# The dense products of a two-layer encoder: 576 tokens in parts of 304 and 272 columns in place of 288 and 288

## The reference

```python
def token_mix(xn, past, w_in, b_f, w_branch, w_gate, w_out):
    (a_q, a_k, a_v, i_q, i_k, i_w, b_q, b_k, b_v, c_q, c_k, c_v, c_f) = split(xn @ w_in)   # 1024 -> 3k columns
    ...                                                                                   # three mixers: o_a, o_b, o_c
    branch = einsum('btnw,nwd->btnd', o, w_branch)                                         # 3 x (512 -> 1024)
    gate = sigmoid((xn @ w_gate).reshape(B, T, 3, 1024))                                   # 1024 -> 3072
    return einsum('btnd,btnd->btd', gate, branch) @ w_out, new_rows                        # 1024 -> 1024

def conv_ffn(xn, conv_past, w_up, conv_w, conv_b, w_down):
    h = xn @ w_up                                                                          # 1024 -> 5632
    hc = conv_b + sum(conv_w[i] * shifted(h, i) for i in range(3))
    g, u = split(hc, 2)
    return (silu(g) * u) @ w_down, last_rows                                               # 2816 -> 1024

def trunk(x, ...):
    for l in range(2):
        x = x + token_mix(rmsnorm(x, norm_mix[l]), ...)
        x = x + conv_ffn(rmsnorm(x, norm_ffn[l]), ...)
    return rmsnorm(x, norm_final), new_state
```

## Time and profile before

| what | value |
|---|---|
| median of three timed runs | 2106.25 us |
| the profiled execution: span from first to last instruction | 2104.0 us |
| mean granted TensorE clock | 0.999 of 2.4 GHz |
| PE busy | 2086.9 us, 99% of the span, 15926 matmuls |
| PE weight loads | 1983.6 us, 94% |
| DVE, ACT, POOL busy | 66%, 48%, 11% |
| DMA | 175.05 MB, 83 GB/s on average |

### The profile page before, as it was taken

How to read it: one execution, slowest core, us unless ns; L and a number is a source line. 1 busy time by engine, 2 the same in 40 slices (tenths; PEclk the granted TensorE clock), 3 DMA queues, 4 the chain that set the end, 5 groups by cost and what they waited for, 6 DMA issues and landing times.

```text
span 2104.0 us, 39764 instructions
## 1 busy us (share of the span) xinstructions
PE 2086.9 (99%) x15926; PEld 1983.6 (94%) x15934; DVE 1395.2 (66%) x2612; ACT 1006.0 (48%) x1635; POOL 228.9 (11%) x162
## 2 busy tenths in 40 slices
PE   8999999999999999999999999999999999999998
PEld 8898988898999999999998989889989999999998
DVE  7669637878747763676465895488787377637753
ACT  6267325647626652444352672255475266424432
POOL 0022000000041110011310220000001301001112
PEclk9999999999999999999999999999999999999999
DMA  6231222121122222222232212221211222222222
GB/s 203 77 106 41 91 81 96 51 81 51 61 81 81 80 90 91 90 80 90 91 108 81 93 44 93 78 96 51 81 51 61 81 89 81 90 91 80 90 85 93
DMA packets 53764, 175.05 MB, mean 83 GB/s; under 512 B 6720, under 2 KB 11408, under 8 KB 53632
## 3 DMA queue, kind: packets, MB, share of 16 engines
q1 hardware_dynamic: 47168, 158.88, 24.0%
q0 software_dynamic: 2688, 9.95, 1.2%
q10 hardware_dynamic: 3776, 4.34, 0.6%
HBM read 160.25 MB, written 12.90 MB: 82 GB/s over the span
## 4 chain that ended last, share of the span: by engine, by line
PE 99%; ACT 0%; DVE 0%; DMA 0%; issue 0%; DVEq 0%; SPq 0%; ACTq 0%
PE d L1499 63%; PE d L1547 15%; PE ab L1593 4%; PE d L1881 2%; PE d L1558 2%; PE d L1890 2%; PE ab L1820 1%; PE ab L1832 1%; PE d L1736 1%; PE d L1597 1%; PE ab L1869 1%; PE ab L1499 1%; PE ab L1814 0%; PE ab L1645 0%; PE ab L1676 0%; PE d L1693 0%
## 5 line engine op out<-in xcount | busy, mean ns | idle before, releaser
L481 ACT ACTIVATE wh<-raw 128x512 fp32r<-128x512 f32 x548 | 345.7, 632 | 717.5 <-PE d L1499 563.9
L853 DVE TENSOR_TENSOR wl<-raw,wh 128x512 fp32r<-128x512 f32 x548 | 388.5, 710 | 303.4 <-ACT wh L481 294.7
L1499 PE MATMUL d<-xh,wh 128*128 128x288 f32 x2400 | 513.8, 295 | 6.9 <-DVE wl L851 6.9
L1499 PE MATMUL d<-xl,wh 128*128 128x288 f32 x2400 | 511.3, 294 | 0.0
L1499 PE MATMUL d<-xh,wl 128*128 128x288 f32 x2400 | 511.0, 293 | 0.0
L1499 PEld LDWEIGHTS d<-xh,wh 128*128 128x128 f32 x2400 | 383.1, 188 | 11.3 <-issue 10.2
L1499 PEld LDWEIGHTS d<-xl,wh 128*128 128x128 f32 x2400 | 383.0, 188 | 0.0
L1499 PEld LDWEIGHTS d<-xh,wl 128*128 128x128 f32 x2400 | 383.0, 188 | 0.0
L1547 PE MATMUL d<-xh,wh 128*128 128x288 f32 x768 | 173.6, 307 | 0.0
L1547 PE MATMUL d<-xh,wl 128*128 128x288 f32 x768 | 164.6, 295 | 0.0
L1547 PE MATMUL d<-xl,wh 128*128 128x288 f32 x768 | 164.3, 295 | 0.0
(11 more groups left out here) (321 smaller groups left out, 3300.7 us busy)
## 6 DMA issues: line engine op xcount, KB each, us to landing
raw<-in_w SPq DMA_DIRECT2D x286, 512.0 KB, 3.5
out_o_k<-k POOLq DMA_DIRECT2D x4, 1152.0 KB, 7.2
out_o_v<-v POOLq DMA_DIRECT2D x4, 1024.0 KB, 8.9
x<-in_xT SPq DMA_DIRECT2D x8, 288.0 KB, 5.8
k<-in_bc_k_past ACTq DMA_DIRECT2D x4, 512.0 KB, 4.2
v<-in_bc_v_past ACTq DMA_DIRECT2D x4, 512.0 KB, 5.2
out_y<-z SPq DMA_DIRECT2D x4, 432.0 KB, 2.7
raw<-in_w SPq DMA_DIRECT2D x4, 256.0 KB, 6.1
```

Source lines behind the costliest of these rows:

```text
L481: act.activation(wh[:, c % SPLIT_SLOTS, :], stored, ACT.Copy).then_inc(high_done, 1)
L853: dve.tensor_tensor(lows, stored, highs, ALU.subtract).then_inc(low_done, 1)
L1499: ins = pe.matmul(outs[half], w_, r_[:, kk, HALF * half:HALF * half + HALF], start=first and n == 0 and begin, stop=last and n == len(kks) ...
```

## The change

`HALF` is replaced by `CUT` = 304 and two slices, `PARTS` = 0:304 and 304:576. Every place that took 288 and 288 columns now takes 304 and 272: the two matmuls of each product, their PSUM places (part 0 still ends at a bank's end, part 1 begins the next), the sums of squares, and the ends by parts on ACT, DVE and SP. No instruction is added, removed or put elsewhere: on each engine the list is the same with other widths. Operations over the whole row of 576 read the same number of columns from a start 16 columns lower in PSUM. The numbers of lines after line 37 are higher by one, after L363 equal again. The diff, cut to its core (L1547, L1558 and the rows marked as left out change in the same way):

```diff
@@ -34,7 +34,8 @@
 TS = 64
 T = TP + TS
-HALF = T // 2
+CUT = 304
+PARTS = (slice(0, CUT), slice(CUT, T))
@@ -215,13 +216,13 @@
-        dv = [d[:, 512 - HALF:512 + HALF] for d in dbank]
-        dhalf = [[d[:, 512 - HALF:512], d[:, 512:512 + HALF]] for d in dbank]
-
-        norm_out = [ab[:, 0, 512 - HALF:512], ab[:, 1, 0:HALF]]
...
-        iq1_out = [ab[:, 2, 512 - HALF:512], ab[:, 3, 0:HALF]]
...
+        dv = [d[:, 512 - CUT:512 - CUT + T] for d in dbank]
+        dhalf = [[d[:, 512 - CUT:512], d[:, 512:512 - CUT + T]] for d in dbank]
+
+        norm_out = [ab[:, 0, 512 - CUT:512], ab[:, 1, 0:T - CUT]]
...
+        iq1_out = [ab[:, 2, 512 - CUT:512], ab[:, 3, 0:T - CUT]]
...
@@ -359,8 +360,7 @@
                     sp.wait_ge(y_ready, 3 * half + n + 1)
-                    a = HALF * half
-                    sp.dma_start(y[:, i:j, a:a + HALF], z[:, i:j, a:a + HALF]).then_inc(st_y, 16)
+                    sp.dma_start(y[:, i:j, PARTS[half]], z[:, i:j, PARTS[half]]).then_inc(st_y, 16)
@@ -812,7 +812,7 @@
             def prescale(half, j):
-                part = slice(HALF * half, HALF * half + HALF)
+                part = PARTS[half]
...
@@ -1453,16 +1453,16 @@
             def end_half(half):
 
-                part = slice(HALF * half, HALF * half + HALF)
+                part = PARTS[half]
...
             def final(half, a, b):
 
-                part = slice(HALF * half, HALF * half + HALF)
+                part = PARTS[half]
                 dve.wait_ge(prescaled, KD * half + b)
-                root = rstd[:, part].unsqueeze(1).broadcast_to((P, b - a, HALF))
+                root = rstd[:, part].unsqueeze(1).broadcast_to((P, b - a, part.stop - part.start))
...
@@ -1496,7 +1496,7 @@
                     for w_, r_, first, last in ((hi_w, rh, True, False), (hi_w, rl, False, False), (lo_w, rh, False, True)):
                         for half in range(2):
-                            ins = pe.matmul(outs[half], w_, r_[:, kk, HALF * half:HALF * half + HALF],
+                            ins = pe.matmul(outs[half], w_, r_[:, kk, PARTS[half]],
                                             start=first and n == 0 and begin, stop=last and n == len(kks) - 1 and end)
...
@@ -1504,7 +1504,7 @@
-                return pe.matmul(norm_out[half], cf[:, C_ONE:C_ONE + P], squares[:, HALF * half:HALF * half + HALF], start=start, stop=stop)
+                return pe.matmul(norm_out[half], cf[:, C_ONE:C_ONE + P], squares[:, PARTS[half]], start=start, stop=stop)
...
@@ -2008,7 +2008,7 @@
-                        ins = pe.matmul(dhalf[d % 2][half], w_, r_[:, kk, HALF * half:HALF * half + HALF],
+                        ins = pe.matmul(dhalf[d % 2][half], w_, r_[:, kk, PARTS[half]],
                                         start=first and kk == 0, stop=last and kk == FH - 1)
```

More of the change, by code:

```diff
@@ L216, in encoder @@
         ab = ctx.enter_context(nc.psum_tensor("ab", [P, 4, 512], F32))
-        dv = [d[:, 512 - HALF:512 + HALF] for d in dbank]
-        dhalf = [[d[:, 512 - HALF:512], d[:, 512:512 + HALF]] for d in dbank]
-        norm_out = [ab[:, 0, 512 - HALF:512], ab[:, 1, 0:HALF]]
-        norm_both = ab[:].rearrange("p a b -> p (a b)")[:, 512 - HALF:512 + HALF]
-        iq1_out = [ab[:, 2, 512 - HALF:512], ab[:, 3, 0:HALF]]
-        iq1_both = ab[:].rearrange("p a b -> p (a b)")[:, 1536 - HALF:1536 + HALF]
+        dv = [d[:, 512 - CUT:512 - CUT + T] for d in dbank]
+        dhalf = [[d[:, 512 - CUT:512], d[:, 512:512 - CUT + T]] for d in dbank]
+        norm_out = [ab[:, 0, 512 - CUT:512], ab[:, 1, 0:T - CUT]]
+        norm_both = ab[:].rearrange("p a b -> p (a b)")[:, 512 - CUT:512 - CUT + T]
+        iq1_out = [ab[:, 2, 512 - CUT:512], ab[:, 3, 0:T - CUT]]
+        iq1_both = ab[:].rearrange("p a b -> p (a b)")[:, 1536 - CUT:1536 - CUT + T]
         turned_small = ab[:, 0, 0:5 * TURNED]
@@ L827, in _ @@
                 prescale(half, KD - 1)
-                rsqrt_of(2 * LAYERS + 1 + half, slice(HALF * half, HALF * half + HALF))
+                rsqrt_of(2 * LAYERS + 1 + half, PARTS[half])
         @block.vector
@@ L1546, in gate_blocks @@
                         for half in range(2):
-                            ins = pe.matmul(dhalf[d][half], w_, r_[:, kk, HALF * half:HALF * half + HALF],
+                            ins = pe.matmul(dhalf[d][half], w_, r_[:, kk, PARTS[half]],
                                             start=first and kk == 0, stop=last and kk == KD - 1)
@@ L1558, in products @@
                         ins = pe.matmul(dhalf[(d + j) % 2][half], weights[:, (c + j) % SPLIT_SLOTS, kk * P:kk * P + P],
-                                        heads[:, kk, HALF * half:HALF * half + HALF], start=first, stop=last)
+                                        heads[:, kk, PARTS[half]], start=first, stop=last)
                     return ins
```

## The result

The changed kernel takes 2141.6 us (median of four runs, 2141.19 to 2141.88) against 2106.32 us (2105.15 to 2106.74). The ratio is 1.0168, with a 95% interval from 1.0155 to 1.0182: 1.7% slower, and outside the range of the prediction. The profiled execution took 2141.19 us at a span of 2139.4 us, 35.4 us over the span before.

What follows compares the result with a forecast made beforehand. PE was taken to bound the kernel through distances between matmul starts. MLP at zero and mixers at 11.5 us less took the 2104.0 us span to 2092.5; adding 2.25 gave about 2095 us, 0.5% faster, range 2081 to 2137.

Steps and rivals of the forecast that it cites:

- PE alone sets the time, through the distances between starts: Whole kernel: PE busy 99% of the span, other engines hidden, so time is the sum of distances between matmul starts.
- MLP stages at 260 a pair, a change of zero: MLP stages: 6270 matmuls keep 260 ns a pair under the new widths, so their time changes by zero.
- short rhythm: Steady spacing of matmul starts at 260 ns a pair (130.0 a matmul), seen before the change in MLP stages.
- Mixer stages to 131.25 a matmul, 11.5 us less: Mixer stages: 6230 matmuls go from a mean of 133.1 to 131.25 ns each, saving 11.5 us.
- The end, between -0.3 and +0.2 us: Sums of squares, end products, last copies and stores: together between -0.3 and +0.2 us, taken as zero.
- The floor: Rival: 272 columns still take 130 ns for fresh weights, 304 take 138.5, so 268.5 a pair, 2140 us; chance 0.14.
- The slip of the MLP into the long rhythm: Rival: MLP stages go to 266.7 ns a pair, adding 20.9 us, 2127 us with mixers unchanged; chance 0.20.
- long rhythm: Steady spacing of matmul starts at 266.7 ns a pair (133.3 a matmul), seen before the change in mixer stages.
- The all-short case: Rival: mixers also go to 130.0 ns a matmul from 133.1, saving 19.3 us, 2087 us; chance 0.18.
- The 122.5 ns beside the rows: Skill's warm gap for 288 columns, columns over 2.4 GHz plus 2.5 ns; by it pair and time would not change.

Runs made afterwards that it cites:

- read288_w304: Against the changed kernel (304/272), the dense products' second part is read from column 288 instead of 304, widths and PSUM places kept; 2118.69 us.
- cut272: The changed kernel's two widths in the other order, 272 columns first and then 304; 2109.7 us.
- weights_shifted_304: The changed kernel (304/272) with an unused tile of 16 columns in front of the split weights, moving them 64 bytes against the activations; 2110.66 us.
- cut320: Parts of 320 and 256 columns throughout, in place of the 288 and 288 of the kernel before; 2123.55 us.
- mixers272: The kernel before with only the mixers' dense products in 272 and 304 columns, MLP and norms kept at 288/288; 2120.34 us, ratio 1.0069.
- mixers256: The kernel before with only the mixers' dense products in 256 and 320 columns, MLP and norms kept at 288/288; 2095.91 us, ratio 0.9951.

## Why the prediction was wrong

- *PE alone sets the time, through the distances between starts.* Right. No wait came, and the 35.4 us are found in these distances to 0.3 us.
- *MLP stages at 260 a pair, a change of zero.* This is the step that failed. The argument was that the short rhythm repeats after a pair, and that a pair stays whole under the cut. It repeats after a pair, but the pair's price isn't a sum of columns: it depends on where the reads of its two parts start against the weights, and on the widths besides. The cut moved the second part's start from column 288 to 304 and brought the dearest MLP price of all runs, 268.9 in place of 260; the term that was put at zero cost 27.9 us. With the start put back to 288 under the new widths (read288_w304) the MLP costs 13.9 us less than that and still 13.9 us more than before, so the start doesn't account for all of it.
- *Mixer stages to 131.25 a matmul, 11.5 us less.* Also wrong, in sign: 134.4, and 7.2 us more. The mean rate of the rows of 512 and 384 columns was taken for a price by columns. cut272 and weights_shifted_304, with the same columns, do come to 131.7, close to the 131.25 of the forecast: the widths did not rule it out, the place did. The base of the term was rough too: it took 132.7 ns for all gate matmuls from a group of 30, while groups of 24 in the same chain take 3.18 to 3.39 us, 132.5 to 141 ns a matmul.
- *The end, between -0.3 and +0.2 us.* It was +0.3; nearly right and without weight.
- *The rivals.* The floor's 2140 us comes within 2 us of the result, by luck, with the wrong mechanism: it wanted 138.5 and 130 ns and 141.3 and 127.3 were measured, and in cut320 a shorter second part than 272 is followed after 116.9. The prediction's range stopped at 2137, short of this rival's own price. The slip of the MLP into the long rhythm named the right stage, and mixers272 shows that such a slip exists and costs what was worked out (2119 expected, 2120.34 measured), but in the changed kernel there is a third rhythm, dearer than both. The all-short case isn't a fancy either: two of the three kinds of long mixer pieces in mixers256 run at 260 to 260.5 a pair, though with other widths.
- *The 122.5 ns beside the rows.* The Trainium skill, "TensorE: Matmul & The Clock Gate", section "Back-to-back issue gap", gives the formula behind them for the isolated matmul and not for a stream in which weight loads and matmuls take turns. This stream is of the second kind, so its 130.0 and 133.3 ns don't contradict the formula, and the formula gives no rival here.
- *What was in the profile and not used.* Two prices for the same columns, in the two streaks of 96 at 130.0 and 133.9 under one line as well, already said that columns alone don't set the price. They don't say what does. But from there, asking what the cut moves besides columns (a start, by 16 columns) would have put more weight on a new price for the MLP, up or down.

What stays open is the mechanism below the distance. The runs show that the price depends on the distance between activations and weights, modulo 256 bytes where that was tried, and on the widths. That the two reads hinder each other is the reading that fits; no run shows it directly, nor in what part of the memory it would be, and no formula here gives the price of a pair that hasn't been run. What starts 288/288 in one rhythm or the other, beyond that the stage before can decide it, wasn't settled.

## What to carry to other kernels

Where matmuls stream without a wait, read their price as piece length over count from the chain, stage by stage; if the same shapes show two prices, the place of the operands against each other may be a knob, and a 64-byte pad in front of a weight buffer tests it in one line. A cut of a token row is a change of read places as much as of widths, so try both orders of two widths. A stage's price can hang on the stage before it: measure a local change over the whole program.

## What was not expected of the hardware

Moving the weights by 64 bytes against the activations changed the whole program by 31 us (2141.6 to 2110.66), and by 9 us the other way with 288/288 (2106.32 to 2115.61). The Trainium skill says in "TensorE: Matmul & The Clock Gate", section "Step-by-step: what each phase is for", that loading the next tile's weights takes no SBUF read bandwidth from the running matmul; these runs measure no bandwidth, but for float32r operands they speak against a load that leaves the stream of matmuls alone, since its price changes with where the weights lie against the activations.

All prices seen in long pieces lie between 260 and 268.9 ns a pair, and the two MLP pieces of one run agree to 0.1 ns: 8 to 12% over the 240 ns that the prediction worked out for 576 columns at 2.4 GHz, with a granted clock of 1.00 in the stretches before the end. And two of them, 260 and 266.7, belong to one and the same MLP code with the same places, each kept for 400 us, and only what the mixers before it ran was changed.

The prices come with short repeating patterns of starts. In the MLP of the kernel before, matmuls are followed after 128 and 132 ns in turn; in mixers272 the same MLP goes 140, 131, 131 and 132, a repeat of two pairs; in the changed kernel it is three pairs. The long rhythm is thus a stall of some 9 ns on every fourth matmul.
